# A decoder layer on one core: the bias lines' products one chunk of gates later, and the later branch weights fetched by GpSimd's queue

## What is computed

```python
h = rms_norm(x, norm_mix_g)
proj = h @ w_in            # queries, keys, values of four mixers, and 4 x 1024 gate columns
o_swa, o_fox, o_sb, o_dsa = four attention mixers, each (1024, 256)
g_swa, g_fox, g_sb, g_dsa = split(sigmoid(gate_cols), 4)
merged = (g_swa * (o_swa @ wb[0]) + g_fox * (o_fox @ wb[1])
          + g_sb * (o_sb @ wb[2]) + g_dsa * (o_dsa @ wb[3]))
x = x + merged @ w_out
y = hierarchical_moe(rms_norm(x, norm_ffn_g), ...)   # 32 experts, two per token
x = x + y
```

## Time and profile before

| what | value |
|---|---|
| runs, median (lowest to highest) | 1799.78 us (1796.22 to 1802.88) |
| the profiled execution, its own time | 1804.91 us |
| its span, first to last instruction | 1803.3 us |
| mean granted clock of TensorE | 0.979 of full speed |
| busy: TensorE, VectorE, ScalarE, GpSimd | 95%, 70%, 48%, 19% |
| stage 2, TensorE's start and end | about 322 to 673 us |
| merge, TensorE's start and end | about 940 to 1041 us |
| experts | about 1160 to 1803 us |

### The profile page before, as it was taken

The page is one execution under the profiler, slowest core; times in us unless marked ns, Lnnn a source line. Parts: engine busy times, 40 slices in busy tenths (PEclk is TensorE's granted clock), DMA queues, the critical chain, the costliest instruction groups (busy, mean ns, idle before and its releaser), DMA issues. The chain is left out here.

```text
span 1803.3 us, 25241 instructions
## 1 busy us (share of the span) xinstructions
PE 1706.3 (95%) x8639; PEld 1405.0 (78%) x8639; DVE 1269.5 (70%) x1697; ACT 860.2 (48%) x1035; POOL 350.7 (19%) x292
## 2 busy tenths in 40 slices
PE   7999999899999998899999999688999999999995
PEld 5887778687888877799986778556888888888774
DVE  4023678799999608777647853497888888888884
ACT  6115542211111214567851011346777777777773
POOL 3111122232222210100000000165222222222221
PEclk9999999899999998999999999889999999999998
DMA  5236233332222437346605644488999999999992
GB/s 194 97 112 171 80 130 117 134 118 93 94 94 93 124 98 170 83 106 132 153 13 210 246 152 176 190 298 299 376 369 372 358 363 352 351 356 353 366 354 76
DMA packets 110578, 361.72 MB, mean 201 GB/s; under 512 B 18731, under 2 KB 22827, under 8 KB 110496
## 3 DMA queue, kind: packets, MB, share of 16 engines
q1 hardware_dynamic: 97508, 342.52, 54.8%
q0 software_dynamic: 12992, 18.14, 4.2%
HBM read 315.51 MB, written 63.96 MB: 210 GB/s over the span
## 5 line engine op out<-in xcount | busy, mean ns | idle before, releaser
L1793 DVE TENSOR_TENSOR ex_wl<-ex_raw,ex_wh 128x2048 fp32r<-128x2048 f32 x192 | 436.9, 2289 | 86.4 <-ACT ex_wh L1789 84.6
L1789 ACT ACTIVATE ex_wh<-ex_raw 128x2048 fp32r<-128x2048 f32 x192 | 367.2, 1915 | 99.7 <-PE ex_upp L2384 37.0
L83 PE MATMUL gs_banks<-hT_hi,gs_wh 128*128 128x512 f32 x512 | 200.7, 392 | 0.0
L84 PE MATMUL gs_banks<-hT_lo,gs_wh 128*128 128x512 f32 x512 | 200.1, 391 | 0.0
L85 PE MATMUL gs_banks<-hT_hi,gs_wl 128*128 128x512 f32 x512 | 199.9, 390 | 0.0
L802 ACT ACTIVATE gs_wh<-gs_raw 128x1024 fp32r<-128x1024 f32 x30 | 31.8, 1061 | 259.9 <-PE gs_banks L85 259.9
L866 DVE MATCH_REPLACE8 selm<-sg_top,selm 128x512 f32<-128x512 f32 (+5 forms) x160 | 139.0, 877 | 0.0
L862 DVE MAX8 sg_top<-selm 128x8 f32<-128x512 f32 (+5 forms) x160 | 134.2, 881 | 0.0
L1643 PE MATMUL at_ops<-at_v,at_pT 128*128 128x65 f32 (+1 forms) x984 | 125.5, 270 | 1.0 <-DMA at_v<-vtok 1.0
L1643 PEld LDWEIGHTS at_ops<-at_v,at_pT 128*128 128x128 f32 x984 | 120.8, 193 | 2.1 <-DMA at_v<-vtok 1.4
L746 POOL TENSOR_TENSOR gs_wl<-gs_raw,gs_wh 128x1024 fp32r<-128x1024 f32 x30 | 73.1, 2437 | 245.4 <-ACT gs_wh L802 245.4
(11 more groups left out here) (336 smaller groups left out, 3687.3 us busy)
## 6 DMA issues: line engine op xcount, KB each, us to landing
ex_raw<-in_w_expert_up SPq DMA_DIRECT2D x128, 1024.0 KB
ex_raw<-in_w_expert_down SPq DMA_DIRECT2D x64, 1024.0 KB
gs_raw<-in_w_gate SPq DMA_DIRECT2D x32, 512.0 KB, 3.4
gatesT<-sg_go SPq DMA_DIRECT2D x32, 512.0 KB, 2.6
selm<-gatesT SPq DMA_DIRECT2D x32, 512.0 KB, 6.3
at_qk<-qkh SPq DMA_DIRECT2D x52, 256.0 KB
at_qk<-qkl SPq DMA_DIRECT2D x44, 256.0 KB
gs_raw<-in_w_qk SPq DMA_DIRECT2D x17, 512.0 KB, 4.9
```

What stands on the lines that cost most here:

```text
L83: pe.matmul(out, a_hi, b_hi, start=(k == 0), stop=False)
L84: pe.matmul(out, a_hi, b_lo, start=False, stop=False)
L1789: act.activation(ring.wh[r][:, :, :], ring.raw[slot][:, :, :], ACT.Copy).then_inc(ring.w_high, 1)
L1793: dve.tensor_tensor(ring.wl[r][:, :, :], ring.raw[slot][:, :, :], ring.wh[r][:, :, :].bitcast(F32), ALU.subtract).then_inc(ring.w_low, 1)
```

## The change

Two edits that have nothing to do with each other.

1. In stage 2, TensorE makes the two bias line products, with their waits for the small loads, behind chunk 1's product instead of ahead of it.
2. In the merge, the branch weights of chunks 2 to 7 are fetched by GpSimd's queue instead of SyncE's. GpSimd waits for the same event (`multiplied`) as SyncE did. SyncE's loop is left with the gate and `w_out` fetches, and no wait on `multiplied`. ScalarE waits for a new semaphore of these fetches, `wb_late`, and no longer for `multiplied` beside it.

```diff
@@ select_and_gate, TensorE @@
-                if k == 0:
+                if k == 1:
                     pe.wait_ge(small_loaded, 32)
                     pe.wait_ge(table_set, 2)
                     for v in range(2):
@@ mix @@
         wb_loaded = [sem(f"mg_wb_loaded{s}") for s in range(2)]
+        wb_late = [sem(f"mg_wb_late{s}") for s in range(2)]
@@ mix, SyncE @@
             for n in range(4, NP):
                 k, j = divmod(n, NB)
-                if j == 0 and k + 1 < KC:
-                    sp.wait_ge(multiplied, n)
-                    load_wb(k + 1)
                 sp.wait_ge(gated, n - 3)
                 load_gate(n)
@@ mix, GpSimd @@
                 pool.tensor_tensor(lo, raw, hi.bitcast(F32), ALU.subtract).then_inc(o_low, 1)
+            for k in range(2, KC):
+                pool.wait_ge(multiplied, NB * (k - 1))
+                pool.dma_start(wb[k % 2].raw[:, :], a["w_br"][k]).then_inc(wb_late[k % 2], 16)
@@ mix, ScalarE @@
             def wb_hi(k):
-                act.wait_ge(wb_loaded[k % 2], 16 * (k // 2 + 1))
-                if k >= 2:
-                    act.wait_ge(multiplied, NB * (k - 1))
+                if k < 2:
+                    act.wait_ge(wb_loaded[k], 16)
+                else:
+                    act.wait_ge(wb_late[k % 2], 16 * (k // 2))
```

## The result

| | before | after |
|---|---|---|
| runs, median (lowest to highest) | 1799.78 us (1796.22 to 1802.88) | 1788.66 us (1784.37 to 1789.98) |
| ratio, 95% interval | | 0.9931 (0.9911 to 0.9951) |
| the profiled execution, its span | 1803.3 us | 1782.8 us |
| TensorE's first operation of stage 3 | 677.7 us | 670.8 us |
| first to last multiplication with j = 0 in the merge | 943.1 to 1033.3 us, 90.2 us | 936.2 to 1017.5 us, 81.3 us |

The changed kernel is faster by 11.1 us as a difference of medians, by 12.4 us from the ratio (8.8 to 16.0 by its interval). The forecast was 1784.5 us, in a range from 1779 to 1796. The direction and the range held; the gain came out at about 11 to 12 us instead of 15.3.

What follows compares the result with a forecast made beforehand. The prediction took TensorE, busy 95% of the span, as the bound, idling at stage 2's start and in the merge. 6.3 + 9.0 = 15.3 us off the median 1799.8 gave 1784.5 us, range 1779 to 1796.

Steps and rivals of the forecast that it cites:

- Bias lines: Start of stage 2: moving the bias lines behind chunk 1 lets chunk 2 start earlier, 6.3 us gained, bounds 4.4 to 6.9.
- VectorE's delay: Stage 2: VectorE gets the bias lines some 5 us later, at no cost, since it idles 66.0 us at stage end.
- Merge: Merge: without SyncE's wait TensorE's waits and slow restarts go, 9.0 us gained, bounds 7.8 to 9.9.
- The floor: Merge: TensorE's 28 undisturbed products take 78.4 us instead of 88.3, so at most 9.9 us can be won.
- They were held by SyncE's wait on TensorE's product: Merge: gates were issued late, though their buffers were free, because SyncE waited for a product only the branch weights need.
- The fetch on GpSimd's queue: Merge: 512 KB of branch weights on GpSimd's queue land in 5.5 us, against 4.2 us on SyncE's own.
- The price beyond the slack: Merge: fetches cost nothing up to a landing at 6.8 us; beyond about 7.5, six cost 6 L - 42.9 us.
- Fetches held off by VectorE: Merge rival: descriptors wait 2.5 us for two VectorE operations, loss 5.1, total gain 11.1, 1788.7 us; chance 0.08.
- Lockstep: Merge rival: small mutual waits of VectorE and TensorE, about 0.6 us per chunk, total gain 12.0, 1787.8 us; chance 0.14.
- Only a swapped wait: Stage 2 rival: chunk 2's low part comes later, TensorE idles until about 341, gain 10.5, 1789.3 us; chance 0.07.
- Late fetch: Merge rival: GpSimd's transfers land late and block VectorE, then TensorE; 1813 us at a landing of 12 us; chance 0.06.
- The sum: Whole kernel: 6.3 + 9.0 = 15.3 us gained, 0.85%, from the median 1799.8 to 1784.5 us.

Runs made afterwards that it cites:

- add_7us: The kernel before with 31 extra matmuls in stage 2, whose sum nothing reads, 7.19 us of TensorE work; 1812.29 us, ratio 1.007.
- before_look_1: The unchanged kernel before, profiled a second time to see its own scatter; this one execution took 1802.92 us.
- queue_hold: queue_only with SyncE's wait on TensorE's product put back ahead of the gates, fetching nothing there; 1793.31 us, ratio 0.9965 to the kernel before.
- fetch_late: The changed kernel with GpSimd's six fetches also waiting for VectorE's first multiplication of the chunk; 1808.43 us, ratio 1.0053 to the kernel before.
- bias_only: The kernel before with the first edit alone, bias lines behind chunk 1; 1795.76 us, ratio 0.9975.
- queue_only: The kernel before with the second edit alone, branch weights of chunks 2 to 7 from GpSimd's queue; 1794.29 us, ratio 0.9966.
- sp_reordered: The kernel before with SyncE issuing the branch weights behind the chunk's third gate, GpSimd's queue left alone; 1793.34 us, ratio 0.996.
- bias_at_2: The changed kernel with the bias lines behind chunk 2 instead of chunk 1; one profiled execution, span 1787.9 us.

## Why the prediction was right, and where it was not

- **Bias lines, 6.3 us forecast.** Right in mechanism and nearly in size: 6.7 us at stage 3's start by the means of the profiles. Chunk 2 was to start at 335.8 to 336.8 and did at 335.70. The forecast allowed for a slow restart behind some 1.5 us of idle time; TensorE idled 1.01 us and kept its clock. Its reason, that 1.5 us is shorter than the 2.26 us that had slowed the restart, is weaker than it looked: add_7us has a slow stretch behind 1.77 us of idle time and before_look_1 none behind 2.60. VectorE's delay cost nothing, as said: 55.0 us of its cover are left.
- **Merge, 9.0 us forecast; the term that was mis-sized.** The floor was right: 28 products were to take 79.3 us, and from the fetch at 946.06 to the end of TensorE's last product at 1025.05 they took 79.0. The 88.3 us that this was taken from were wrong as a base. They came from one execution, whose merge was 1.6 us longer than the mean of five. With the mean the term is 7.3, from the first to the last multiplication with j = 0.
- **"They were held by SyncE's wait on TensorE's product".** As the whole reason this step failed. With the wait put back and the branch weights gone from ahead of the gates, the merge is 81.5 us instead of 81.3. The wait uses up the gates' lead, 3.4 to 4.0 us instead of 9.1 to 11.5, and the landing behind 512 KB on the same queue, 1.4 us later by the mean and 2.3 us at the boundary of the earlier trace rows, is what then comes out as a wait. That the forecast survived this is luck: the edit takes both away.
- **The fetch on GpSimd's queue.** 5.5 us taken, 5.0 measured; VectorE at the low part 8.0 us behind the product by the forecast, 965.05 - 957.27 = 7.8 measured. The price beyond the slack had the right threshold (free at 6.3 to 6.8 us in queue_hold), and gave only 10.5 of the 19.4 us where the fetch hung on VectorE.
- **Fetches held off by VectorE** (0.08): the trace has GpSimd's issues at 0.53 to 0.59 us while VectorE is busy 64.82 of 73 us, and the landing at 5.0 us. No hold-off shows. The rule of the Trainium skill's page "SBUF — State Buffer", section "Summary: rules for kernel authors", does not apply to VectorE's operations here, as the forecast read it, and the trace agrees with that.
- **Lockstep** (0.14) would have left 0.6 us at each boundary; TensorE's waits for VectorE sum to 1.4 us in three places. **Only a swapped wait** (0.07) fell with chunk 2's start at 335.70. **Late fetch** (0.06) did not occur, but fetch_late shows it 1.4 us away.
- **The sum.** By the profiles it is 6.7 + 7.3 = 14.0 us instead of 15.3. The timed runs show 11.7 (9.4 to 14.0) and 12.4 (8.8 to 16.0), so 14.0 lies at the upper end of the one interval and inside the other. The shortfall of some 2 us sits in bias_only: 4.5 us timed (2.5 to 6.3) against 6.7 at stage 3. The merge's part is there nearly in full, 6.1, 6.3 and 7 us timed in queue_only, queue_hold and sp_reordered. The prediction's own range should by its terms have begun at 1799.8 - 16.8 - 2 = 1781, not at 1779; nothing hangs on it. Why the first edit's gain shrinks behind stage 3 stays open: the clock in the attention varies by more than that from run to run, but that it does so more often with this edit was not shown.

## What to carry to other kernels

When a small, urgent transfer comes late, look at two things together: what holds its issue back, and which bytes are released at the same moment ahead of it in the same queue. Here either alone was harmless, the hold because the transfer still landed just in time, the bytes because the lead was long; undoing one of them is enough, and undoing both leaves slack (in the changed kernel the gates land 4.4 to 7.9 us before their use). Work that must be done somewhere is free inside a wait that can't be avoided; one step later it costs its length, and in the one execution seen a slow restart on top. Before a gain is sized from waits for DMAs, profile the kernel more than once: here one execution overstated it by 1.6 of 9 us.

## What was not expected of the hardware

- Within one queue, a 512 KB transfer issued 0.38 us ahead delayed the landing of the next by 1.4 us in the mean of six places (5.0 against 3.6 us) and by 2.3 us in the worst, against the same transfer at the same moment on another queue. There the other one paid: it landed in 6.5 us instead of 5.0. The same transfer issued 1.3 to 2.8 us ahead in one queue (sp_reordered) left the next at 3.7 to 5.3 us, as in the changed kernel (3.8 to 5.2).
- The length of an idle time alone did not decide on TensorE's clock. Behind 1.01 and 1.27 us it went on at matmuls of 0.40 us, but also behind 2.60 and 2.65 us (before_look_1, fetch_late); behind 1.77 (add_7us), 2.26 and 2.68 us (bias_at_2) it went down to its lower level, matmuls of 0.63 us, for about 3 us. In bias_at_2 the first five matmuls behind the gap were still quick and the slow ones came 1.3 us after the restart.
- The same program was granted a clock of 1.00, 0.91 or 0.79 over the same 40 us of the attention in three executions, with no cause visible in the trace. The 0.79 went with some 5 us more of attention (270.8 against 265.4), the 0.91 with none (265.6).
